# A decoder layer's branch gates: from 16 column units to seven block products per branch

## The reference

```python
mod = (silu(c) @ ada_w + ada_b).reshape(B, 6, D_MODEL)   # c: (1, 1024), ada_w: (1024, 6144)
h = rms_norm(x, mix_norm_g) * (1 + scale_m) + shift_m    # (256, 1024)
proj = h @ w_in      # pool 256, sg 512, conv 512, q/k/v 256 each, f 4, gates 4 x 1024
ys = stack([y_pool, y_sg, y_conv, y_att])                # 4 branches, (256, 256) each
branch = einsum('bsnc,ncd->bsnd', ys, w_branch)          # w_branch: (4, 256, 1024)
gates = sigmoid(gate_cols).reshape(B, S, 4, 1024)
merged = sum(gates * branch, axis=branches)
x = x + gate_m * (merged @ w_out)                        # w_out: (1024, 1024)
x = x + gate_f * moe(rms_norm(x, ffn_norm_g) * (1 + scale_f) + shift_f)
```

## Time and profile before

| | us |
|---|---|
| three runs | 769.02, 770.3, 770.35 |
| median | 770.3 |
| the profiled execution, its own time | 770.35 |
| its span | 768.5 |
| PE busy in the span | 726.7 |
| DVE, ACT, POOL busy | 337.0, 169.4, 37.5 |
| mean bandwidth of all transfers | 353 GB/s |

### The profile page before, as it was taken

One profiled execution on the slowest core, in us unless ns is written; L12 is line 12 of the kernel. 1 busy time (PEld: TensorE's weight loads), 2 busy tenths in 40 slices (PEclk: granted clock), 3 DMA queues, 4 the chain that ended last, 5 costly groups with the idle time before them and its releaser, 6 DMA issues.

```text
span 768.5 us, 12356 instructions
## 1 busy us (share of the span) xinstructions
PE 726.7 (95%) x4982; PEld 380.5 (50%) x4982; DVE 337.0 (44%) x793; ACT 169.4 (22%) x341; POOL 37.5 (5%) x30
## 2 busy tenths in 40 slices
PE   4899999899999999999999999999999997999894
PEld 1588888788887444333343333433333342333231
DVE  1108694885568686333335333331333332332234
ACT  3213330200000333222222222221222221222113
POOL 0200001111113100000000000000000000000000
PEclk9999999999999999999999999999999998999998
DMA  9999635768879688999999999999999999999992
GB/s 338 380 350 364 222 104 201 237 227 293 259 236 407 246 333 287 387 422 419 412 385 423 420 420 419 411 419 421 420 421 421 411 416 421 420 420 421 414 403 98
DMA packets 78470, 271.46 MB, mean 353 GB/s; under 512 B 4984, under 2 KB 33792, under 8 KB 57808
## 3 DMA queue, kind: packets, MB, share of 16 engines
q1 hardware_dynamic: 76848, 264.78, 88.4%
q0 software_dynamic: 1264, 5.79, 2.0%
q10 hardware_dynamic: 304, 0.13, 0.1%
HBM read 269.62 MB, written 1.05 MB: 352 GB/s over the span
## 4 chain that ended last, share of the span: by engine, by line
PE 74%; DMA 16%; DVE 4%; SPq 3%; ACT 1%; issue 1%; POOLq 0%; ACTq 0%; DVEq 0%
PE bank L1167 73%; DMA ring<-exp_w_dram 13%; DMA ring<-w_in_dram 2%; SPq L369 2%; PE bank L1527 1%; SPq L372 1%; DMA reg<-reg 1%; DVE part L798 0%; DVE reg L933 0%; DVE reg L1104 0%; DVE reg L1101 0%; ACT reg L671 0%; DVE bank L1120 0%; PE bank L1256 0%; DVE reg L1000 0%
## 5 line engine op out<-in xcount | busy, mean ns | idle before, releaser
L1167 PE MATMUL bank<-ring,h_hT 128*32 128x512 f32 (+2 forms) x2112 | 263.9, 592 | 9.6 <-DMA ring<-exp_w_dram 9.6
L1167 PE MATMUL bank<-h_hT,ring 128*128 128x256 f32 x704 | 156.7, 381 | 1.5 <-DMA ring<-w_in_dram 1.5
L1167 PEld LDWEIGHTS bank<-ring,h_hT 128*32 128x32 f32 (+1 forms) x2112 | 81.2, 114 | 151.3 <-issue 132.3
L1167 PEld LDWEIGHTS bank<-h_hT,ring 128*128 128x128 f32 x704 | 134.1, 191 | 21.3 <-ACT h_hT L514 1.9
L1167 PE MATMUL bank<-ring,const_misc 128*32 128x512 f32 x1008 | 116.5, 595 | 3.2 <-ACT const_misc L678 2.2
L1120 DVE TENSOR_TENSOR bank<-bank,reg 128x512 f32<-128x512 f32 x64 | 44.4, 694 | 62.2 <-PE bank L1167 62.2
L1124 DVE TENSOR_TENSOR y_part<-bank,y_part 128x512 fp32r<-128x512 f32 x64 | 44.3, 691 | 42.4 <-ACT y_part L686 21.2
L1167 PEld LDWEIGHTS bank<-ring,const_misc 128*32 128x32 f32 x1008 | 30.5, 110 | 64.5 <-issue 61.4
L1101 DVE TENSOR_TENSOR reg<-reg,bank 128x256 f32<-128x256 f32 x32 | 13.5, 421 | 102.2 <-ACT reg L671 102.2
L671 ACT ACTIVATE reg<-bank 128x256 f32<-128x256 f32 x32 | 12.3, 385 | 204.3 <-PE bank L1167 204.3
L798 DVE SCALAR_TENSOR_TENSOR part<-ring,cact,part 128x512 f32<-128x512 f32 x56 | 51.3, 915 | 1.9 <-DVE part L798 0.2
(11 more groups left out here) (237 smaller groups left out, 468.5 us busy)
## 6 DMA issues: line engine op xcount, KB each, us to landing
ring<-exp_w_dram SPq DMA_DIRECT2D x155, 1024.0 KB, 14.9
ring<-exp_w_dram SPq DMA_DIRECT2D x67, 512.0 KB, 13.7
ring<-ada_w_dram SPq DMA_DIRECT2D x24, 1024.0 KB, 12.8
ring<-w_in_dram SPq DMA_DIRECT2D x24, 1024.0 KB, 12.1
ring<-w_branch_dram SPq DMA_DIRECT2D x4, 1024.0 KB, 13.1
ring<-w_out_dram SPq DMA_DIRECT2D x4, 1024.0 KB, 8.0
ring<-shared_w_dram SPq DMA_DIRECT2D x2, 1024.0 KB, 14.4
spare<-exp_w_dram SPq DMA_DIRECT2D x2, 1024.0 KB, 14.7
```

The costliest lines, as they stand in the source:

```text
L1167: return pe.matmul(o, lhsT, rhs, start=start, stop=stop, skip_group_check=True)
```

## The change

Write a branch's gate columns as a product of `hT` (two token blocks by two halves of the 1024 inputs) and the 1024x1024 weight (two input halves by two halves of 512 columns). The change computes this 2x2 by 2x2 block product by seven block products instead of eight (Winograd's form). A unit is now one block of the weight, 512 rows by 512 columns, `B11`, `B12`, `B22`, `B21`. The four sums of token blocks (`h_sum`) are made once by VectorE. Of the four sums of weight blocks of each branch, two are made by transfers that GpSimd issues: `B12 += B11` in its ring slot, and `w_sum`, a second copy of `B12` loaded from HBM into `x_sb`, to which `B22` is added; the other two (`sum_2`, `sum_4`) by VectorE over 2048 columns. ScalarE copies three products out of PSUM and VectorE combines (`combine`); the third and fourth token sums and products carry turned signs, so two gate tiles take sigmoid(-x). The loops run over branches n, all four tiles of a branch together. The gates now have tokens on partitions, so `branch` and `merge` do too, and `merged` is turned on TensorE (`turn_merged`) and copied by ScalarE before the output projection. Since `w_sum` overwrites x, x is loaded again later.

The late conditioning units are 256 rows by 1024 columns, two steps of 1024 each; a vector of 1024 is complete after four units and then takes two all-reduces. Of the convolution's 31 taps nine now stand ahead of the forget gate's first read, 14 behind it, 4 after the gelu inputs, 4 between combines. The attention's turned probabilities overwrite `prob`; some semaphores are merged.

```diff
 def unit_plan():
     units = [("ada", i) for i in range(8)] + [("mix", i) for i in range(8)]
-    for g in range(N_GATE):
-        if g % 4 == 3:
-            units.append(("branch", g // 4))
-        units += [("gate", g), ("ada", 8 + g)]
+    for n in range(NB):
+        units += [("gate", 4 * n + b) for b in range(4)]
+        units += [("ada", N_EARLY + 4 * n), ("ada", N_EARLY + 4 * n + 1), ("branch", n)]
+        units += [("ada", N_EARLY + 4 * n + 2), ("ada", N_EARLY + 4 * n + 3)]
...
+            if kind == "gate":
+                last = {B11: P_6, B12: P_5, B22: P_3, B21: P_4}[i % 4]
+                return S["prod_done"], N_P * (i // 4) + last
...
+            def sums_3_1(n):
+                if n:
+                    pool.wait_ge(S["prod_done"], N_P * (n - 1) + P_7)
+                    pool.wait_ge(S["t_done"], N_S + N_T * (n - 1) + T_2)
+                pool.dma_start(w_sum.rearrange("p (k n) -> p k n", k=4), source(("gate", 4 * n + B12))).then_inc(S["t3_in"], 16)
+                arrived(n, B11)
+                arrived(n, B12)
+                pool.dma_start(b_block(n, B12), b_block(n, B11), accum_op=ALU.add).then_inc(S["t1_in"], 16)
+                arrived(n, B22)
+                pool.wait_ge(S["t3_in"], 32 * n + 16)
+                pool.dma_start(w_sum, b_block(n, B22), accum_op=ALU.add).then_inc(S["t3_in"], 16)
...
+            pool.wait_ge(S["unit_done"], 1)
+            sums_3_1(0)
+            sums_3_1(1)
             pool.wait_ge(S["sg_y"], 1)
...
+            sums_3_1(2)
+            cast(0)
+            cast(1)
+            cast(2)
+            cast(3)
+            sums_3_1(3)
+            cast(4)
+            cast(5)
+            pool.wait_ge(S["prod_done"], N_P * (NB - 1) + P_7)
+            pool.wait_ge(S["t_done"], N_S + N_T * (NB - 1) + T_2)
+            pool.dma_start(x_sb[:, :, :], a["x"][0].rearrange("(b p) d -> p b d", p=P)).then_inc(S["late_in"], 16)
+            cast(6)
+            cast(7)
...
+            for n in range(1, NB):
+                copy_p1(n)
+                gate_tile(n, 0, C_11)
+                copy_p7(n)
+                copy_x(n)
+                gate_tile(n, 1, C_22)
+                gate_tile(n, 2, C_12)
+                gate_tile(n, 3, C_21)
...
+            act.wait_ge(S["cast_done"], 8)
             leading(0)
...
+            token_sums()
+            dve.wait_ge(unit_read[1], 1)
+            conv_taps(0, CONV_EARLY)
             dve.wait_ge(S["f_done"], 1)
...
+            sum_2(0)
+            sum_4(0)
+            combine(0, C_11)
+            combine(0, C_T)
+            conv_taps(CONV_MORE, TAPS)
+            combine(0, C_22)
...
+            accumulate(1)
+            for n in range(1, NB):
+                first = [1, 2, 7, 12][n]
+                if n > 1:
+                    cast_out([0, 0, 1, 4][n])
+                accumulate(first)
+                sum_2(n)
+                combine(n, C_11)
+                sum_4(n)
+                if n > 1:
+                    cast_out([0, 0, 2, 5][n])
+                accumulate(first + 1)
+                combine(n, C_T)
+                if n == 2:
+                    cast_out(3)
+                accumulate(first + 2)
+                combine(n, C_22)
+                accumulate(first + 3)
+                combine(n, C_12)
+                if n == 1:
+                    cast_out(0)
+                if n < 3:
+                    accumulate(first + 4)
+                combine(n, C_21)
+                for q in range(4):
+                    merge(n, q)
+            cast_out(6)
...
+            def product(b, lhs, rhs, fresh, last):
+                rhs = rhs.rearrange("p (k n) -> p k n", k=4)
+                for k in range(4):
+                    ins = mm(bank[b][:, :], lhs[:, k, :], rhs[:, k, :], fresh and k == 0, last and k == 3)
+                ins.then_inc(S["prod_done"], 1)
...
+            def product_7(n):
+                pe.wait_ge(S["t3_in"], 32 * (n + 1))
+                product(3, h_sum[:, 2, :, :], w_sum, True, False)
...
+            def product_3(n):
+                ready(("gate", 4 * n + B22))
+                pe.wait_ge(S["c_done"], N_C * n + C_T)
+                product(2, h_sum[:, 3, :, :], b_block(n, B22), False, True)
...
+            def branch(n, q):
+                if q == 0:
+                    ready(("branch", n))
                     pe.wait_ge(*[(S["pool_y"], 2), (S["sg_y"], 1), (S["conv_y"], 1), (S["av_y"], 1)][n])
+                if n == 0 and q < 2:
+                    pe.wait_ge(*[(S["av_y"], 1), (S["sg_y"], 1)][q])
+                else:
+                    pe.wait_ge(S["gb_done"], 4 * n + q - 1)
...
+            def turn_merged(tb):
+                pe.wait_ge(S["merged_done"], 10 + 2 * tb)
+                for k in range(KD):
+                    ins = pe.transpose(bank[2 * tb + k // 4][:, k % 4 * P:(k % 4 + 1) * P], merged[:, tb, k * P:(k + 1) * P], ident)
...
+            for n in range(NB):
+                product_1(n)
+                if n == 0:
                     attend()
+                product_2(n)
+                product_7(n)
+                product_5(n)
+                if n == 0:
                     spatial()
                     pool_linear()
+                product_6(n)
+                product_3(n)
+                if n == 0:
                     pe.wait_ge(S["conv_done"], 2 * TAPS)
                     channel_sum(bank[7], conv, S["csum_done"])
+                product_4(n)
+                if n == 0:
+                    pe.wait_ge(S["conv_var"], 1)
                     pe.wait_ge(S["pool_y"], 2)
+                    channel_sum(bank[6], sq_c, S["csum_done"])
+                branch(n, 0)
+                branch(n, 1)
+                branch(n, 2)
+                if n == NB - 1:
+                    turn_merged(0)
+                branch(n, 3)
```

More of the change, by code:

```diff
@@ L328, in linker, with a_block, b_block @@
             return link
+        def a_block(tb, kb):
+            return hT[:, 4 * kb:4 * kb + 4, tb * P:(tb + 1) * P]
+        def b_block(n, b):
+            return unit(("gate", 4 * n + b))
         def source(u):
             kind, i = u
+            if kind == "ada" and i >= N_EARLY:
+                c = LATE_ROWS[(i - N_EARLY) // 4] * D
+                q = (i - N_EARLY) % 4
+                return a["ada_w"][0, q * 256:(q + 1) * 256, c:c + D].rearrange("(k p) n -> p k n", p=P)
             if kind == "ada":
@@ L364, in _ @@
                     sp.wait_ge(*used_up(BEFORE[u]))
+                    kind, i = BEFORE[u]
+                    if kind == "gate" and i % 4 == B11:
+                        sp.wait_ge(S["t_done"], N_S + N_T * (i // 4) + T_4)
                 src = source(u)
@@ L587, in _ @@
             act.wait_ge(S["av_done"], 1)
             act.activation(y[:, 3, :, :].rearrange("p j t -> p (j t)"), bank[4][:, :], ACT.Copy).then_inc(S["av_y"], 1)
[L590 to L600, removed]
+            copy_p7(0)
@@ L753, in _, with conv_taps @@
                               sig_c[:, :, :], ALU.mult).then_inc(unit_read[1], 1)
+            def conv_taps(first, last):
+                for i in range(first, last):
+                    for j in range(2):
+                        w = pr("conv_w", j * TAPS + i, j * TAPS + i + 1)
+                        src = glu[:, j, i:i + T]
+                        if i:
+                            dve.wait_ge(S["conv_done"], 2 * i + j - 1)
+                            ins = dve.scalar_tensor_tensor(out=conv[:, j, :], in0=src, scalar=w, in1=conv[:, j, :],
+                                                           op0=ALU.mult, op1=ALU.add)
+                        else:
+                            ins = dve.tensor_scalar(conv[:, j, :], src, w, pr("conv_b", j, j + 1), ALU.mult, ALU.add)
+                        ins.then_inc(S["conv_done"], 1)
@@ new lines, in accumulate @@
+            def accumulate(i):
+                v, q = i // 4, i % 4
+                u = ("ada", N_EARLY + i)
+                w = unit(u).rearrange("p (k n) -> p k n", k=2)
+                acc = row_acc[v % 2]
+                dve.wait_ge(landed[SLOT[u]], 16 * (FILLS[u] + 1))
+                if q == 0 and v >= 2:
+                    dve.wait_ge(S["cast_done"], 2 * (v - 1))
+                for k in range(2):
+                    at = cact[:, 2 * q + k:2 * q + k + 1]
+                    if q or k:
+                        dve.wait_ge(S["acc_step"], 2 * i + k)
+                        ins = dve.scalar_tensor_tensor(out=acc, in0=w[:, k, :], scalar=at, in1=acc, op0=ALU.mult, op1=ALU.add)
+                    else:
+                        ins = dve.tensor_scalar(acc, w[:, k, :], at, None, ALU.mult)
+                    ins.then_inc(S["acc_step"], 1)
+                dve.wait_ge(S["acc_step"], 2 * i + 2)
+                dve.sem_inc(S["acc_done"], 1)
@@ new lines, in sum_2, with sum_4 @@
+            def sum_2(n):
+                dve.wait_ge(S["t3_in"], 32 * (n + 1))
+                dve.wait_ge(S["t1_in"], 16 * (n + 1))
```

(15 more changed lines are left out.)

309 lines of the change are left out of this document (181 added, 128 removed).

## The result

The changed kernel takes 780.67 us (median of four runs, 779.69 to 782.12), the kernel before, beside it, 769.66: ratio 1.0142 [1.0129, 1.0154]. It is slower by 11 us, where 762.5 and a gain were forecast; the time lies above the range. The profiled execution took 782.12, with a span of 780.3 (before 768.5).

What follows compares the result with a forecast made beforehand. TensorE was taken to bound the mixer's second half and release the transfer-bound expert stream. Gain 16.8, less 7.1 of waits and 1.9 of slow stretch, is 7.8 off 770.35: 762.5 us, range 752.5 to 770.5.

Steps and rivals of the forecast that it cites:

- The step that failed: Phase n=1: VectorE's last combine waits for cast 0, behind n=2's third block landing near 150.5; TensorE waits 2.8 us.
- the waits of n=2: TensorE waiting for VectorE in phase n=2: 0.7 before P3 and 3.6 at the merges, 4.3 us.
- the slow stretch: Slow TensorE products after a wait, like the one at 147.89; one of two candidates charged, 1.9 us (0.85 + 1.07).
- the gain of 16.8 without waits: TensorE's full gain: 13.8 from gate products, minus 1.8 for turning `merged`, plus 4.8 for wait, slow stretch and hand-overs.
- the wait for `conv_y`: TensorE's wait for the convolution goes, its branch coming third; with slow stretch and hand-overs worth 4.8 us.
- the expert stream tied to the fourth output block: Expert loads wait for the fourth output block, ending at 271.44; moving that moves the whole stream and the end.
- rival 4: Gates' gain is there, but the expert stream, not tied to 271.44, takes it back: 770 us; chance 0.05.
- Rival 1: VectorE keeps up: all-reduces fall where it waits anyway, or 1024-wide steps cost less than 1.28; 753.5 us; chance 0.18.
- rival 3: VectorE later: all-reduces block it for 3.58 each, or wide sums exceed 2.3; 772.5 us; chance 0.10.
- Rival 2: Accumulating transfers slow, so the weight sums arrive after P7 is due; at 30 us each 788.5, break-even near 23; chance 0.09.
- the cover: Products hiding third-sum transfers until P7 (product with `w_sum`): issued about 115, 151, 189; 22, 20 and 18 us.
- My 6 to 10 us for a landing: Each 1 MB accumulating SBUF transfer lands in 6 to 10 us, from a plain load's 5.0, hidden behind products.

Runs made afterwards that it cites:

- Experiment 1: The changed kernel with cast 0 (GpSimd's first all-reduce) put between the load of `w_sum` and the waits for branch 2's weight blocks; 769.57 us, ratio 1.0001.
- experiment 2: The changed kernel with the 1 MB load of `shared_w2` moved behind the last all-reduce; 778.44 us, ratio 1.0107.
- experiment 3: The changed kernel with its eight accumulating transfers made plain copies, the weight sums left out of the computation; 776.24 us, ratio 1.0087.
- experiment 4: The changed kernel with the nine moved convolution taps put behind the forget gate again; 782.98 us, ratio 1.0176.
- experiment 8: Experiment 1 with its eight accumulating transfers made plain copies, the weight sums left out of the computation; 758.64 us, ratio 0.9872.
- experiment 5: Experiment 1 with VectorE's first conditioning unit of n=1 taken early, at 94 us; 770.43 us, ratio 1.0022.
- experiment 6: Experiment 5 with the 1 MB load of `shared_w2` moved behind the last all-reduce; 767.81 us, ratio 0.9978.
- experiment 9: Experiment 6 with branch 0's two conditioning units loaded ahead of its four weight blocks; 761.13 us, ratio 0.9901.
- experiment 10: Experiment 9 with two of the bias loads issued later; 762.18 us, ratio 0.9901.
- experiment 11: Experiment 10 with two weight sums per branch added by GpSimd in eight steps, without second load or accumulating transfers; 792.66 us, ratio 1.0307.
- experiment 7: Experiment 6 with ScalarE copying the block into `w_sum` instead of a second HBM load, and two bias loads issued later; 779.68 us, ratio 1.0139.

## Why the prediction was wrong

**The step that failed** is in the phase n=1: "behind the third block of n=2, which SyncE issues only at `acc_done` 4, about 146, and which lands near 150.5". The wait had been seen and its place named; the landing was taken from a row of nearly empty queues (share 0.08 from 110 to 120 us), although the same text counts 5.2 MB more from HBM and 8 MB of accumulation. The issue came as forecast, at 145.69; it landed at 163.28, 12.8 us later than forecast. Behind it stands the first all-reduce, which I priced at 3.58 as any other; ahead of it are 6.08 us more, a term that the sum put at nothing. In the kernel before, the first all-reduce stands behind an idle stretch of 20.44 us, in which such a time does not show:

```profile
...
142.11 3.50 POOL L482 PARTITION_ALL_REDUCE cond<-part  x1 [20.44 <-DVEq L803]
...
```

12.8 + 6.1 = 18.9, and TensorE's wait is 21.6 in place of 2.8, 18.8 more. Experiment 1 takes both off TensorE's path with the order alone.

What those 6 us are, no trace shows: the profile has no instruction in them and nothing that ends them. They stand before the first all-reduce alone: 6.08 here, 5.99 to 6.19 in experiments 2, 3, 4 and 8, 6.74 to 9.39 in experiments 1, 5, 6, 9 and 10; why it is longer there stays open. In experiment 11 such idle time does not come once only: from the first all-reduce on it stands at each change between additions and all-reduces, 6.23 to 9.32 us.

**The balance.** Forecast for the fourth output block 263.6; +18.8 by that wait; -1.6 since the waits of n=2 are 1.05 + 1.49 + 0.20 = 2.7, not 4.3; +1.2 since the slow stretch is 3.06 (6.49 - 3.43), not 1.9. Sum 282.0, measured 282.16. (The 1.9 was itself misread. In the kernel before, TensorE has one wait between 94.51 and 271.34, the 2.52 us at 147.89. Behind it eight halves take 2.58 us start to start against 1.73 at 158.28, which is the 0.85; the granted clock is 0.50 from 149 to 152 us and 1.00 again from 152.5. The 1.07 compares a row's duration, 7.97, with a start to start; start to start the unit behind 150.47 takes 7.81 against 6.91, so the old stretch cost 0.85 + 0.90 = 1.75.)

**Right:** the 3.43 of a product; the gain of 16.8 without waits (experiment 9: the fourth output block ends 8.8 us earlier than before, at 262.58, with 5.8 us of waits and 2.3 of slow steps behind them, 16.9 in all); units at 1.28 a step, 128x2048 sums at 2.3, 1.86 lost beside an all-reduce (4.46 for 2.60 at 174.10); the wait for `conv_y` gone; the expert stream tied to the fourth output block. So rival 4 falls. Rival 1 falls by the waits of experiment 9, rival 3 by VectorE's prices.

**Rival 2** is half right. Its mechanism does not show in the changed kernel, where the wait of 21.6 comes first and gives the sums time; it shows as soon as that one goes (8.36 in experiment 1), and experiments 1 and 8 price the accumulation at 10 to 11 us of the kernel's time. Its break-even of 23 us is not reached by any landing (11.0 to 15.9 in the changed kernel, up to 17.7 in experiment 7), yet P7 waits: the cover was counted from an issue at 151, and that came at 163.28. My 6 to 10 us for a landing were too low, by a third and more.

**Not settled:** why an accumulating megabyte holds the queues for twice the time of a plain one (2.5 us, an estimate from 1.05 MB at the 412 GB/s of experiment 8, and 2.5 more). No run separates what such a transfer reads from what it writes. None ran alone: the nearest is branch 1's first sum, issued at 110.37 at the end of the idle stretch with one load beside it, and it landed in 11.4 us, as a plain copy in 8.5 (experiment 8). And that the slow stretch belongs to the wait is seen, not tested: the granted clock was 0.50 of the full one from 170 to 180 us, with TensorE idle, and 0.70 from 180 to 190: 0.50 up to 186, while the two projections took their 6.49 us, and 0.98 to 1.00 behind it.

```profile
...
170.00:180.00 10.00, 0.00 (x0) 0.00 (x0) 6.31 (x5) 0.55 (x1) 7.36 (x2) 0.50 1.01 294
180.00:190.00 10.00, 9.93 (x17) 4.24 (x18) 6.52 (x10) 0.08 (x1) 0.00 (x0) 0.70 0.79 292
...
```

## What to carry to other kernels

Price a landing by what is in the queues when the transfer is issued: add up the bytes of every queue from the last idle stretch on, and look for an idle stretch into which loads can be moved. On an in-order engine put what another engine waits for ahead of a wait for data, and ask of every step added to a queue what it stands behind; one reordered line was worth 11 us here, the order of two loads, one megabyte less and one unit taken early, together, another 8. GpSimd's first all-reduce, and each change between additions and all-reduces, stood behind 6 to 9 us that no wait explains (5.99 to 9.39 in ten of the kernels, 6.23 to 9.32 in experiment 11): let the first run where nobody waits, and do not alternate.

## What was not expected of the hardware

- An accumulating SBUF transfer of 1 MB takes 2.5 us more of all queues than a plain copy and lands in 11 to 16 us in the changed kernel; while it ran in experiment 1, the queues showed full share (1.06) at 262 GB/s, where experiment 8 has 1.02 at 412. So the busy share does not tell the rate.
- Additions by GpSimd (128x512, both inputs in SBUF) take 1.3 to 1.9 us each (5.00 to 7.43 for four) and stretched eight two-input taps of VectorE from 0.40 to 1.29 us each (7.1 lost in 10.35, where an all-reduce costs 1.86 in 3.58). A sum over 2048 columns that VectorE started at 110.23, just ahead of the first addition at 110.25, kept its 2.29; one that started at 191.62 in the changed kernel, just behind an all-reduce at 191.51, took 4.28.
- On GpSimd a change between additions and all-reduces cost 6.23 to 9.32 us each time (experiment 11).
